# A hybrid attention and expert layer: DVE order at the output projection's end, two loads held instead of six, last scatter in half rows, a running sum of softplus rows, and fetches that leave out rows at weight zero

## What is computed

```python
# token mixing: stick-breaking attention (8 heads of 64, strictly causal)
log_1m = where(before, log_sigmoid(-z), 0.0)          # z = q k^T / 8
csum = cumsum(log_1m, axis=-1)
log_a = log_sigmoid(z) + (csum[..., -1:] - csum)      # a sum over all later keys before t
a = where(before, exp(log_a), 0.0);  o_a = a @ v
# beside it: sparse attention whose keys an indexer picks (top 128 of each row), then
x = x + gate1 * ((sigmoid(g_a) * (o_a @ w_o_a) + sigmoid(g_b) * (o_b @ w_o_b)) @ w_out)
# channel mixing: 16 experts of width 512, each token goes to 2 experts of one group of 4
h2 = rmsnorm(x) * (1 + scale2) + shift2
probs = softmax(h2 @ router_w + router_b)             # best group, top 2 in it
hidden = silu(h2 @ w_gate[e]) * (h2 @ w_up[e])        # for the tokens of expert e
x = x + gate2 * combine[e] * (hidden @ w_down[e])
```

## Time and profile before

| | |
|---|---|
| median of 3 runs | 828.36 us (826.06 to 828.86) |
| profiled execution | 832.38 us, its span 830.5 us |
| mean granted TensorE clock | 0.963 |
| PE, DVE, ACT, POOL busy | 92%, 73%, 52%, 13% of the span |
| DMA | 184.93 MB, 223 GB/s over the span |

### The profile page before, as it was taken

One profiled execution on the slowest core, in us unless ns is written; L12 is line 12 of the kernel. 1 busy time (PEld: TensorE's weight loads), 2 busy tenths in 40 slices (PEclk: granted clock), 3 DMA queues, 4 the chain that ended last, 5 costly groups with the idle time before them and its releaser, 6 DMA issues.

```text
span 830.5 us, 9977 instructions
## 1 busy us (share of the span) xinstructions
PE 763.1 (92%) x3628; PEld 588.4 (71%) x3628; DVE 610.1 (73%) x794; ACT 430.8 (52%) x519; POOL 105.5 (13%) x90
## 2 busy tenths in 40 slices
PE   3799999999999979999999966899999999999983
PEld 2587777776666646667888855788888887888862
DVE  4665977622998986553566565889999999999980
ACT  6325134355656434556433342676677777676650
POOL 4020000000000000002000011213132241313111
PEclk9879999999999999999999986999999999999996
DMA  9916998110130131105338236999999999999923
GB/s 295 328 49 261 384 362 310 52 51 1 51 102 1 52 101 46 57 10 204 118 126 333 98 137 232 413 397 374 386 388 388 387 388 387 388 371 378 387 57 55
DMA packets 87307, 184.93 MB, mean 223 GB/s; under 512 B 8112, under 2 KB 27672, under 8 KB 85216
## 3 DMA queue, kind: packets, MB, share of 16 engines
q1 hardware_dynamic: 79200, 156.29, 50.2%
q0 software_dynamic: 8064, 28.09, 11.9%
HBM read 171.74 MB, written 12.62 MB: 222 GB/s over the span
## 4 chain that ended last, share of the span: by engine, by line
PE 58%; DVE 17%; DMA 12%; issue 6%; ACT 5%; SPq 1%; DVEq 1%; POOL 0%; ACTq 0%; POOLq 0%
PE ps L658 14%; PE ps L660 13%; PE ps L659 13%; DMA gx<-rows_scratch,slot_tok 8%; DVE w_lo L1879 7%; PE ps L814 4%; ACT w_hi L1446 2%; DMA raw<-in_w_in 2%; DVE ys L1984 2%; PE ps L796 1%; PE ps L898 1%; PE ps L1061 1%; DVE w_lo L1541 1%; PE ps L926 1%; PE ps L914 1%
## 5 line engine op out<-in xcount | busy, mean ns | idle before, releaser
L1879 DVE TENSOR_TENSOR w_lo<-raw,w_hi 128x2048 fp32r<-128x2048 f32 x80 | 179.5, 2286 | 5.7 <-ACT w_hi L1446 5.7
L1446 ACT ACTIVATE w_hi<-raw 128x2048 fp32r<-128x2048 f32 x80 | 150.9, 1914 | 3.5 <-PE ps L660 3.5
L658 PE MATMUL ps<-act_lo,w_hi 128*128 128x512 f32 x232 | 99.1, 427 | 7.6 <-DVE act_lo L1583 3.6
L658 PE MATMUL ps<-w_lo,hgT_hi 128*128 128x512 f32 x256 | 103.0, 403 | 2.4 <-DVE w_lo L1879 0.7
L659 PE MATMUL ps<-w_hi,hgT_lo 128*128 128x512 f32 x256 | 100.4, 392 | 0.0
L660 PE MATMUL ps<-w_hi,hgT_hi 128*128 128x512 f32 x256 | 100.3, 392 | 0.0
L660 PE MATMUL ps<-act_hi,w_hi 128*128 128x512 f32 x232 | 91.7, 395 | 0.0
L659 PE MATMUL ps<-act_hi,w_lo 128*128 128x512 f32 x232 | 91.6, 395 | 0.0
L1185 ACT ACTIVATE w_hi<-raw 128x2048 fp32r<-128x2048 f32 (+2 forms) x29 | 51.9, 1794 | 68.9 <-DMA raw<-in_w_in 45.8
L1541 DVE TENSOR_TENSOR w_lo<-raw,w_hi 128x2048 fp32r<-128x2048 f32 (+2 forms) x29 | 61.9, 2145 | 32.4 <-ACT w_hi L1185 32.3
L658 PEld LDWEIGHTS ps<-act_lo,w_hi 128*128 128x128 f32 x232 | 44.1, 190 | 33.0 <-issue 16.1
(11 more groups left out here) (273 smaller groups left out, 1389.8 us busy)
## 6 DMA issues: line engine op xcount, KB each, us to landing
raw<-in_w_down SPq DMA_DIRECT2D x32, 1024.0 KB, 13.4
raw<-in_w_gate SPq DMA_DIRECT2D x30, 1024.0 KB, 18.1
raw<-in_w_up SPq DMA_DIRECT2D x18, 1024.0 KB, 17.1
raw<-in_w_in SPq DMA_DIRECT2D x16, 1024.0 KB, 6.5
raw<-in_w_ada SPq DMA_DIRECT2D x16, 1024.0 KB, 7.4
raw_late<-in_w_up SPq DMA_DIRECT2D x14, 1024.0 KB, 15.9
raw<-in_w_ada SPq DMA_DIRECT2D x8, 512.0 KB, 6.7
raw_early<-in_w_ada SPq DMA_DIRECT2D x8, 512.0 KB, 6.1
```

What stands on the lines that cost most here:

```text
L658: pe.matmul(o, a[0], b[1], start=start, stop=False)
L1446: act.activation(e_hi[s_][:, :], e_raw[r][:, :], ACT.Copy).then_inc(e_top, 1)
L1879: dve.tensor_tensor(e_lo[s_][:, :], e_raw[r][:, :], e_hi[s_][:, :].bitcast(F32), ALU.subtract).then_inc(e_split, 1)
```

## The change

- **Running sum.** After `suffix(m)` of blocks 2 and 1 DVE adds the later block's sum in place (`sums`, between the second and the third round of the step), so that `suffix` of blocks 1 and 0 needs one `negones` product for each head instead of two and three. Its `negtri` products come first, then PE waits for the sum.
- **DVE order.** `modulated(2)` and `logit(2)` stand ahead of `residual(1, 3)`, `by_amp(1, 3, 4)` after `rstd(3)`, and `modulated(3)` after `r_sel`.
- **Loads.** Only z = 10 and 11 wait for the first expert's rows.
- **Fetch.** A fourth column of the slot table holds the token number, plus 1024 where the weight is zero. From expert 2 on `fetch` takes its row numbers from there, with a bound of 511 and no error beyond it: those rows are left as they were. `slot_index` has one more copy.
- **Tail.** The last `down` goes by halves of the columns; each half is scaled and scattered by itself (rows of 2 KB; `half_row` holds the row numbers).

```diff
-                    if isinstance(z, int) and 6 <= z < E_RAW:
+                    if isinstance(z, int) and 10 <= z < E_RAW:
                         sp.wait_ge(rows_in[0], 16)
...
+            def scatter_halves(X):
+                halves = out[0].rearrange("s (h d) -> (s h) d", h=2)
+                pool.wait_ge(scat, 16 * X)
+                for h, signal in enumerate((scat_half, scat)):
+                    pool.wait_ge(y_sb, 2 * X + 1 + h)
+                    pool.indirect_dma_start(halves, bass.IndirectOffsetOnAxis(half_row[:, h:h + 1], 0),
+                                            ys[:, 512 * h:512 * h + 512], None, compute_op=ALU.add).then_inc(signal, 16)
...
             def fetch(X):
...
+                if X < 2:
+                    pool.indirect_dma_start(gx[X][:, :], None, rows_d, bass.IndirectOffsetOnAxis(slot_tok[:, X:X + 1], 0)
+                                            ).then_inc(rows_in[X], 16)
+                else:
+                    pool.indirect_dma_start(gx[X % 2][:, :], None, rows_d,
+                                            bass.IndirectOffsetOnAxis(slot_src[:, X % N_EXP:X % N_EXP + 1], 0),
+                                            bounds_check=S - 1, oob_is_err=False).then_inc(rows_in[X % 2], 16)
...
                 for r in range(2):
-                    for j in range(NT - 1, i - 1, -1):
-                        lhs = negtri if j == i else negones
-                        pe.matmul(zt[m % 2][:, r, P * (j - i):S - P * i], lhs[:, :], sp_tile(hp, j)[:, r, :],
+                    pe.matmul(zt[m % 2][:, r, 0:S - P * i], negtri[:, :], sp_tile(hp, i)[:, r, :], start=False, stop=False,
+                              skip_group_check=True)
+                if NT - 1 - i >= 2:
+                    pe.wait_ge(sp_sum, 2 * hp + NT - 2 - i)
+                for r in range(2):
+                    if i < NT - 1:
+                        pe.matmul(zt[m % 2][:, r, P:S - P * i], negones[:, :], sp_tile(hp, i + 1)[:, r, :],
                                   start=False, stop=False, skip_group_check=True)
...
+            def down_last(X, z0, z, turn):
+                pe.wait_ge(hidT_sp, X + 1)
+                pe.wait_ge(y_sb, 2 * X)
+                pe.wait_ge(e_split, z + 2)
+                for n in range(2):
+                    for f in range(4):
...
+            def sums(m):
+                hp, i = STEPS[m]
+                if i not in (1, 2):
+                    return
+                dve.wait_ge(s_ps, m + 1)
+                t = sp_tile(hp, i)
+                dve.tensor_tensor(t[:, :, P:], t[:, :, P:], sp_tile(hp, i + 1)[:, :, :], ALU.add).then_inc(sp_sum, 1)
...
-                topk_rounds(4 if m < 8 else 3)
+                topk_rounds(2)
+                sums(m)
+                topk_rounds(2 if m < 8 else 1)
...
             rstd(2)
+            modulated(2)
+            logit(2)
             residual(1, 3)
-            by_amp(1, 3, 4)
-            logit(2)
...
             rstd(3)
-            modulated(2)
+            by_amp(1, 3, 4)
             logit(3)
-            modulated(3)
...
             dve.tensor_tensor(pr, r_top[:, :, :], bestb, ALU.mult).then_inc(r_sel, 1)
+            modulated(3)
...
+            dve.scalar_tensor_tensor(out=slot_t[:, :, :, 3], in0=comb[:, :, :], scalar=-2.0 * S,
+                                     in1=tid_off[:, :].unsqueeze(2).broadcast_to([P, NT, N_EXP]), op0=ALU.mult, op1=ALU.add)
...
+                dve.tensor_copy(slot_src[:, bass.ds(e + b, 1)], ps[7][:, 4 * b + 3:4 * b + 4])
...
+            def scaled_last(X, e, turn):
+                dve.wait_ge(scat, 16 * X)
+                dve.wait_ge(y_half, turn)
+                scaled_part(e, 0)
+                dve.wait_ge(e_used, EC * X + 6)
+                scaled_part(e, 1)
...
                 stage(X0 + N_EXP - 1, N_EXP - 1, 1, False, False, turn, again)
+                dve.tensor_scalar(half_row[:, 0:1], slot_tok[:, N_EXP - 1:N_EXP], 2.0, None, ALU.mult)
+                dve.tensor_scalar(half_row[:, 1:2], slot_tok[:, N_EXP - 1:N_EXP], 2.0, 1.0, ALU.mult, ALU.add)
                 scaled(X0 + N_EXP - 2, N_EXP - 2, 0)
-                scaled(X0 + N_EXP - 1, N_EXP - 1, 1, True)
+                scaled_last(X0 + N_EXP - 1, N_EXP - 1, turn)
```

More of the change, by code:

```diff
@@ L190, in hybrid_layer @@
     slot_w = at("slot_w", [N_EXP], F32, small[0])
+    half_row = at("half_row", [2], I32, small[0] + 0.0625)
     neg_ge = tiny("neg_ge", [P], BF16)
+    SRC = at("slot_src", [N_EXP], I32, small[0]), at("tid_off", [NT], F32, small[0] + 0.125)
     neg_gt = tiny("neg_gt", [P], BF16)
@@ L342, in hybrid_layer @@
         qk_var, qk_sd, qk_norm = sem("qk_var"), sem("qk_sd"), sem("qk_norm")
-        z_ps, z_soft, sp_ready, s_ps, a_ready = (
-            sem(n) for n in ("z_ps", "z_soft", "sp_ready", "s_ps", "a_ready"))
+        z_ps, z_soft, sp_ready, sp_sum, s_ps, a_ready = (
+            sem(n) for n in ("z_ps", "z_soft", "sp_ready", "sp_sums", "s_ps", "a_ready"))
         oa_ps, oa_hi, oa_sp = sem("oa_ps"), sem("oa_hi"), sem("oa_sp")
@@ L637, in expert_pass @@
                 scatter(X0 + N_EXP - 2)
-                scatter(X0 + N_EXP - 1)
+                scatter_halves(X0 + N_EXP - 1)
             pool.wait_ge(st_rows, 16 * NT)
@@ L646, in _ @@
                     expert_pass(p * N_EXP)
+                pool.wait_ge(scat_half, 16 * PASSES)
                 pool.wait_ge(scat, 16 * PASSES * N_EXP)
+            pool.wait_ge(scat_half, 16)
             pool.wait_ge(scat, 16 * N_EXP)
@@ L1093, in up_chunk, with down @@
                 m.then_inc(e_used, 1)
-            def down(X, z0, z, halves=(0, 1), rest=None):
+            def down(X, z0, z, halves=(0, 1)):
                 if 0 in halves:
@@ L1101, in down @@
                 for h in halves:
-                    if h and rest is not None:
-                        pe.wait_ge(hidT_sp2, rest)
                     pe.wait_ge(e_split, z + h + 1)
@@ L1112, in down @@
                     m.then_inc(e_used, 1)
+            def down_last(X, z0, z, turn):
[4 more added lines that the diff above has]
+                    for f in range(4):
+                        s_ = (z0 + f // 2) % E_SPL
+                        a = D * (f % 2) + 512 * n
+                        if n == 0 and f == 2:
+                            pe.wait_ge(hidT_sp2, turn)
+                        m = three(ps[5 + n][:, :], (hidT_hi[:, f, :], hidT_lo[:, f, :]),
+                                  (e_hi[s_][:, a:a + 512], e_lo[s_][:, a:a + 512]), f == 0, f == 3)
+                        if n == 0 and f == 3:
+                            m.then_inc(y_half, 1)
+                        elif n == 1 and f % 2:
+                            m.then_inc(e_used, 1)
             def turn_hid(X):
@@ L1975, in slot_index, with scaled_part, scaled @@
                 dve.tensor_copy(slot_tok[:, bass.ds(e + b, 1)], ps[7][:, 4 * b:4 * b + 1])
+                dve.tensor_copy(slot_src[:, bass.ds(e + b, 1)], ps[7][:, 4 * b + 3:4 * b + 4])
                 dve.tensor_reduce(slot_w[:, bass.ds(e + b, 1)], ps[7][:, 4 * b + 1:4 * b + 3], AX.X, ALU.add).then_inc(idx_ok, 1)
-            def scaled(X, e, b, last_=False):
-                dve.wait_ge(e_used, EC * X + (6 if last_ else 10))
+            def scaled_part(e, n):
+                dve.scalar_tensor_tensor(out=ys[:, 512 * n:512 * n + 512], in0=ps[5 + n][:, :],
+                                         scalar=slot_w[:, bass.ds(e, 1)], in1=gate2[:, 512 * n:512 * n + 512],
+                                         op0=ALU.mult, op1=ALU.mult).then_inc(y_sb, 1)
+            def scaled(X, e, b):
+                dve.wait_ge(e_used, EC * X + 10)
                 if not isinstance(X, int) or X >= 1:
                     dve.wait_ge(scat, 16 * X)
+                if not isinstance(X, int) and isinstance(e, int) and e == 0:
+                    dve.wait_ge(scat_half, X)
                 for n in range(2):
-                    dve.scalar_tensor_tensor(out=ys[:, 512 * n:512 * n + 512], in0=ps[5 + n][:, :],
-                                             scalar=slot_w[:, bass.ds(e, 1)], in1=gate2[:, 512 * n:512 * n + 512],
-                                             op0=ALU.mult, op1=ALU.mult).then_inc(y_sb, 1)
+                    scaled_part(e, n)
+            def scaled_last(X, e, turn):
[4 more added lines that the diff above has]
+                scaled_part(e, 1)
             def hg_low(X, b):
```

10 lines of the change are left out of this document (6 added, 4 removed).

## The result

The changed kernel takes **837.02 us** (median, 835.98 to 843.99) where the kernel before took 828.61 in the same session (826.06 to 830.52). The ratio is 1.0117, with a 95% interval of 1.008 to 1.0154. I had forecast 820.6. The change is slower by 8.4 us by the medians and by 9.7 by the ratio, where I had forecast 7.8 faster.

A forecast was written before the change was run, and what follows sets the result against it. PE paces stick-breaking with DVE right behind; PE, DVE and DMA are all full in the expert loop; the tail is a chain. Gains 2.4 + 0.1 + 4.3 + 1.0 = 7.8 us took 828.36 to 820.6, range 815.5 to 826.5.

The forecast's parts named there:

- term C: Expert loop: earlier loads and left-out rows make fetches land sooner, ending PE's waits; gain 4.3 us, bounds 0 and 4.9.
- A, running sum: Stick-breaking steps: fewer `negones` products on PE, sums added on DVE, PE waiting for some; gain 2.4 us, not 7.
- Rivals 2 and 3: Running sum on DVE: sums weigh more, loss 0.8, 823.8 us, chance 0.12; or little, gain 5.5, 817.5 us, chance 0.08.
- B, DVE order: Routing: ranks 0.93 us earlier, `counts` 0.45 earlier, 0.38 left after one more copy; with the loads' cost, gain 0.1.
- C, loads: Before the loop: four loads moved from 507.5 to 487.1 us just fit, costing the first fetch 0.3 us.
- rival 4: Loop start: first fetch held by the last store behind the four loads, 3.4 us; total 824.0 us, chance 0.08.
- C, the loop: Expert loop: fetches landing 0.5 us earlier suffice, half the rows left out; gain 4.3 us, bounds 0 and 4.9.
- the left-out rows might be worth nothing: Loop fetches: by the skill's eight partitions per DMA engine, skipping relieves only the last engines; early loads must do everything.
- The prediction's last line: Prediction is wrong if DVE's loop queue turns PE's saved waits into low-part waits, or a third stage eats gains.
- Rival 5: Loop fetches slower as POOL compares every row number with the bound; 8.8 us more, total 833.7 us, chance 0.05.
- D, tail: Kernel's end: last scatter by halves, the second taking 4.8 us instead of 6.2; gain 1.0, bounds gain 2.0, loss 0.4.

The follow-up runs named there:

- breaks: Changed kernel, bounded fetches kept, with three one-element DVE writes between the four `w_lo` in a pair's second expert: 824.10 us, ratio 0.9938.
- sum_alone: Kernel before with the running sum alone: 824.90 us, ratio 0.9959.
- sum_order: Kernel before with the running sum and the new DVE order; loads, fetches and tail as before: 824.29 us, ratio 0.9953.
- all_rows: Changed kernel with every fetch bringing all 128 rows by `slot_tok`, with no bound: 827.09 us, ratio 0.9989.
- loads_alone: Kernel before with only the four loads held no longer (`10 <= z` for `6 <= z`): 828.45 us, ratio 1.0002.
- breaks_whole: Changed kernel with bounded fetches, three one-element DVE writes between the four `w_lo`, and the last scatter in one piece: 822.97 us, ratio 0.9932.
- pool_late: Changed kernel with all rows fetched, no bound, and a small POOL write between a pair's two fetches: 825.67 us, ratio 0.9969.

## Why the prediction was wrong

The step that failed is the term C of 4.3 us. It took for granted that POOL's queue gets through the changed fetches as before. It didn't: second fetches of 9.8 us put 10.5 us on the loop. Two terms were mis-sized besides, the first fetch (0.3 for what cost 2.8) and the tail (a gain of 1.0 for a loss of 0.3). Even with the stall taken away by breaks the gain is 5.1 us (3.2 to 7.0 inside the interval), not 7.8.

**A, running sum: right.** Predicted 2.4. From the first row above to the first rows of the sparse attention it was 126.18 before and is 123.57 after: 2.6. The ratio of sum_alone gives 3.4, with 1.4 to 5.4 inside the interval. Rivals 2 and 3, on the weight of the sums, fall. PE's four waits for the sum were to be 0.8, 0.5, 1.8 and 1.0; they are 0.93, 0.21, 1.35 and 0.92. The last two:

```profile
275.64 0.70 PE L839 MATMUL ps<-sp,negones 128*128 128x256 f32 x2 [1.35 <-DVE sp L1715]
...
282.38 0.91 PE L839 MATMUL ps<-sp,negones 128*128 128x384 f32 x2 [0.92 <-DVE sp L1715]
```

**B, DVE order: right, and small.** `counts` was to come 0.45 earlier; sum_order has it 0.7 earlier than sum_alone (325.40 against 326.06), both counted from the start of stick-breaking and with a granted clock of 0.96 between 290 and 330 us. The ten other profiles with the order and a clock of 0.96 or 1.00 there have 325.1 to 325.5, the three at 0.91 have 326.3 to 326.7.

**C, loads: the step on the first fetch was mis-sized.** I put 0.3 on it, from "it just fits". It cost 2.8. Behind the loads the store of the last rows took 6.2 us to land instead of the 3.9 of the earlier trace rows (2.9 in sum_order, which has the store at the same place and the loads held):

```profile
rows_scratch<-hn POOLq DMA_DIRECT2D x1, 512.0 KB, 6.2
```

The first fetch waited for it, 1.4 later against `counts` than before (5.86 against 4.42). Its bracket names `slot_w`, but the store lands at 489.74 + 6.22 = 495.96 and the fetch starts 0.82 later, the distance that it has behind the store in all_rows and loads_alone too. PE began 5.44 after its issue (496.78 to 502.22) instead of 4.05: another 1.4. Of that 1.26 is time on POOL, and DVE's doing once more. Coming later, the fetch fell into a `w_lo` and took 2.29 us instead of 1.03, until 0.9 after the end of this one:

```profile
495.89 2.28 DVE L1932 TENSOR_TENSOR w_lo<-raw_late,w_hi 128x2048 fp32r<-128x2048 f32 x1
```

This is rival 4, priced there at 3.4 and given 0.08; it had the store right and not the hold on POOL. The error is one of method: I had added up bytes over a stretch of 16 us, while the store waits for what is queued at its own moment, and what is late behind it can meet another engine.

**C, the loop: the step that failed.** The gain I had named, 4.3, is real but smaller: the waits of PE for `gx` between 540 and 780, 2.3 us before, all but vanish (0.3, and 0.7 in all_rows, where all rows are fetched), and with the stall gone the loop is 2.6 to 3.0 us shorter than before (breaks_whole and breaks). That the left-out rows might be worth nothing, which the prediction weighed, isn't borne out in the profiles: with the writes in place they give 2.1 us of the loop with the loads early, 0.8 with them held. But the changed fetch cost 10.5 us in the loop (301.06 to 311.51). I had weighed POOL's busy share, 9.8 us of 37, and concluded that POOL has time. It has; what it hasn't is a free moment of its own choosing, since its indirect DMAs depend on when DVE lets them through. The prediction's last line had the sign, PE's saved waits turning into waits for low parts, but put it down to DVE's queue; here DVE is late because it waits for the scatters. Rival 5 had the right sign for the wrong reason: no comparison with a bound is seen in any duration, PE hardly waits for the fetch but for low parts, two steps behind the scatter that is queued after it, and its price, 8.8 for the 10.5 measured, is near only by chance.

**D, tail: wrong.** Predicted a gain of 1.0; it is a loss of 0.3 by the averages above. Here are the rows of after:

```profile
820.11 1.41 DVE L2035 SCALAR_TENSOR_TENSOR ys<-ps,slot_w,gate 128x512 f32<-128x512 f32 x2 [6.66 <-DMA out<-ys,slot_tok]
821.63 1.54 POOL L629 DMA_INDIRECT out<-ys,half_row  x1 [6.36 <-DVE ys L2035]
823.47 1.54 POOL L629 DMA_INDIRECT out<-ys,half_row  x1 [0.30 <-issue]
```

I had the first half issued 1.05 after the start of `ys`; it takes 1.52, against 1.68 for a whole one. The second half leaves 1.84 behind the first. Counted from scatter 14, the last issue comes 9.6 us later with halves and 8.5 with a whole scatter, on average over the nine and nine profiles: 1.1 later, where I had 0.2. From the last issue to the end of the span it is 11.2 on average with halves (11.8 in this profile) and 12.0 with a whole one. So a half saves 0.8 (0.4 between the profiles of before and after), not the 1.4 I took. The Trainium skill (DMA: Bandwidth & Descriptors, Anatomy of one DMA), weighed in the prediction, gave 0.6 by estimate, nearer to the 0.8 than my 1.4.

What stays open: why a transfer that starts with a run of `w_lo` or up to 0.38 us into it misses three boundaries when DVE has come through without a stop, and none when it stood idle shortly before. sum_alone, sum_order, loads_alone and pool_late have one scatter of 9.2 us each, some 1.16 us into the run, where others at 1.16 to 1.24 take 2.5, all of them with DVE unstopped; what decides there wasn't found. What a one-element write changes there isn't shown, only that with it no transfer missed the first boundary. Whether the shared port is the cause is argued from the skill and from which instructions let a transfer through, not measured.

## What to carry to other kernels

Indirect DMAs on GpSimd are not free work on an idle engine: read their durations beside VectorE's timeline. In this kernel the same transfer took 0.97 in one place and 2.9 in another, its time hung on VectorE, and an edit that moved it by less than a tenth of a microsecond made it 9.8. Where VectorE runs several two-operand SBUF instructions in a row, a one-element instruction between them may be enough. And what is queued behind a slow transfer on GpSimd may be what the others wait for, not the transfer itself.

## What the runs showed of the hardware

- An indirect DMA instruction on GpSimd that meets a two-SBUF-input VectorE instruction ends 0.96 (fetch) or 1.54 us (scatter) after a VectorE boundary; one that started with an unbroken run of four or up to 0.38 us into it, with VectorE unstopped ahead of the run, took 9.4 to 10.0 us (23 of 23) and ended that long after the boundary that closes the run. With VectorE idle shortly before, it took 2.8 to 3.4 (38 of 38).
- A bounds check is seen only as some 0.5 us more between the row numbers and the fetch's start. It made no fetch longer by itself (0.99 to 1.06 with, 0.94 to 1.03 without, out of `w_lo`'s way).
- A scatter of half the bytes, issued 1.84 us behind the other half, took 0.8 us less from issue to the end of the span (averages of nine profiles each: 11.2 and 12.0).
